# Query projection of a sparse attention: one 512-column matmul over high and low x in place of two of 256 columns

## The chip, the cores and the metric

The kernel runs on one core of one Trainium2 chip. Times are device microseconds of one launch. The core has TensorE (matmuls; PE in the profile, its weight loads PEld), VectorE (DVE), ScalarE (ACT), GpSimd (POOL) and SyncE (SP), which issues the DMAs. Each engine works off its own list of instructions in order; semaphores hold them together. PSUM, where matmuls write, has 8 banks of 512 fp32 columns on 128 partitions.

## The reference

A decoder layer on 256 tokens of width 2048, in fp32: an RMS norm, one wide projection, two attentions side by side (latent attention with 8 heads, sparse attention with 16 heads), an output projection, an MLP with squared ReLU, and a last norm. The change touches the projection that gives the sparse attention its queries, 16 heads of 64 features:

```python
n = rmsnorm(h, attn_norm_w[l])
proj = n @ w_in[l]
c_q, c_kv, k_rope, q_nsa, kv_cmp, kv_slc, kv_win, gate_logits = _split_cols(proj, IN_SIZES)
...
q = q.reshape(B, T, G, HG, NSA_DK)
```

so q_nsa is a product of 256 tokens x 2048 by 2048 x 1024. The norm's factor of a token is multiplied in afterwards, to the projected columns.

## The kernel before

Every fp32 product is made of three cheaper ones. A factor is split into a high part (rounded, type fp32r) and a low part (the rest), and high x high, high x low and low x high are summed in PSUM. ScalarE makes the high part of each chunk of weights (`split_hi`, L653), VectorE the low part (`split_lo`, L1010, which subtracts). Chunks of 2048 columns alternate between two places (`w_hi`, `w_lo`), so a chunk's splits wait for TensorE to be done with the chunk two before it (semaphore `w_used`, or `w_half` for half a chunk). x lies turned in SBUF as `xT[128, part, k, token]`, part 0 high and part 1 low.

The queries are made turned, with features on the partitions and the 256 tokens as columns: the weights are the stationary operand and xT moves. There are four parts of 256 features, each from two chunks of weights (8 blocks of k each), listed in `A_IN = (22, 24, 26, 28, 29, 30, 31, 32)`. The function `q_products` does a chunk in four quarters: a half of the blocks (4) and a half of the features (f). For each block it issues three matmuls of 256 columns: high weights with high x (L1896), high weights with low x (L1897), low weights with high x (L1900). Both halves of the features of a part sit side by side in one bank, and part p uses bank p.

The order of the work is the list `PLAN`, which each engine walks through, taking what is its own: ("hi", c) and ("lo", c) are splits of chunk c, ("w", c) is a whole chunk of matmuls and ("q", (c, n)) a quarter of one, ("s", i) a step of the attention, ("k", ...) single pieces. The chunks 21, 23, 25 and 27 (`CMP`) belong to the compression of keys and values and stand between query chunks. From chunk 29 on query quarters alternate with the first steps of the latent attention (scores in banks 4 and 5, turned probabilities in bank 6, results in bank 7); chunk 33 (`WO_M`) begins the output projection, which sums in banks 0 to 3.

Who uses banks 0 to 3 ahead of the queries: the turned keys stand in banks 0 and 1 and are split from there into `k2h` (ScalarE) and `k2l` (VectorE, semaphore `kv_out`, counts 3 and 4); the rotary query pieces stand in banks 2 and 3 and are split into `qs` (semaphore `qs_lo`, counts 1 and 2). A part leaves PSUM in `scale_queries`: VectorE multiplies the bank by `rrow`, the tokens' factors, into `qfa` or `qfb` (L1250, semaphore `q_in`). The pieces ("c", part) then split it into `q2a` or `q2b` (ScalarE L834, VectorE L1010). Parts 0 and 1 are scaled just ahead of their splits, parts 2 and 3 together in ("k", "out"), behind the last query chunk.

## Time and profile before

| | |
|---|---|
| median of 3 runs | 1027.6 us (1027.17 to 1027.95) |
| profiled execution, its own time | 1027.19 us |
| its span in the trace | 1025.4 us |
| TensorE busy | 1013.0 us, 99%, 5547 matmuls |
| weight loads | 879.2 us, 86% |
| VectorE busy | 793.4 us, 77% |
| ScalarE busy | 612.7 us, 60% |
| GpSimd busy | 88.9 us, 9% |
| query matmuls (L1896, L1897, L1900) | 3 x 128, from 117.2 to 181.1 us |

The span is the time from the first to the last instruction in the trace. Busy shares are an average over stages. A matmul's duration in the trace contains its way through the pipeline, so matmuls that follow each other overlap; the time that one takes from the next is the distance between their starts. A releaser (after <-) is the instruction whose semaphore event ended an engine's idle time.

### The profile page before, as it was taken

What the parts mean: (1) busy time and instruction counts of PE and PEld (TensorE: products, weight loads), DVE (VectorE), ACT (ScalarE), POOL (GpSimd) and SP (SyncE); (2) the same over time, 40 slices, a digit from 0 to 9 for tenths busy, and PEclk for the clock granted to TensorE, in tenths of its full rate; (3) what the DMA queues carried; (4) which work ended last, traced back from release to release, by engine and by line L of the source; (5) the groups of instructions that cost most, each with busy time, mean ns of one, the idle gap of its engine ahead of it and who ended that gap; (6) DMA issues with size and microseconds to landing.
All of it is one profiled execution on the core that took longest, in us unless ns stands there. A gap on an engine that the chain in (4) does not pass through costs nothing.

```text
span 1025.4 us, 14183 instructions
## 1 busy us (share of the span) xinstructions
PE 1013.0 (99%) x5547; PEld 879.2 (86%) x5547; DVE 793.4 (77%) x1086; ACT 612.7 (60%) x872; POOL 88.9 (9%) x151
## 2 busy tenths in 40 slices
PE   8999999999999999999999999999999999999996
PEld 7889999888888888888888888888888888888885
DVE  4655886988866589869958968976995996897594
ACT  5655855877764576556646655745655564575433
POOL 2135200632200000000000000000000000000002
PEclk9999999999999999999999999999999999999999
DMA  9576672243236547666666665666666666675553
GB/s 339 184 204 193 207 254 105 89 160 123 83 123 205 159 132 206 202 193 210 190 194 199 204 205 177 210 193 201 206 196 190 192 207 201 186 210 189 195 197 131
DMA packets 182798, 190.84 MB, mean 186 GB/s; under 512 B 9206, under 2 KB 145100, under 8 KB 182348
## 3 DMA queue, kind: packets, MB, share of 16 engines
q1 hardware_dynamic: 182300, 189.41, 58.5%
q8 instruction: 44, 0.72, 0.3%
q10 hardware_dynamic: 432, 0.52, 0.1%
q14 instruction: 22, 0.18, 0.0%
HBM read 187.82 MB, written 2.10 MB: 185 GB/s over the span
## 4 chain that ended last, share of the span: by engine, by line
PE 92%; DVE 4%; ACT 2%; DMA 1%; issue 1%; DVEq 0%; ACTq 0%
PE ps L2048 20%; PE ps L2116 12%; PE ps L2052 10%; PE ps L2123 6%; PE ps L1605 4%; PE ps L1606 4%; PE ps L1609 4%; PE ps L2091 4%; PE ps L2090 4%; PE ps L2097 4%; PE ps L2020 3%; PE ps L1896 2%; PE ps L1897 1%; PE ps L2025 1%; PE ps L1900 1%; PE ps L1880 1%
## 5 line engine op out<-in xcount | busy, mean ns | idle before, releaser
L2048 PE MATMUL ps<-xT,high 128*128 128x512 f32 x896 | 212.7, 390 | 0.2 <-DVE hid L1408 0.2
L2048 PEld LDWEIGHTS ps<-xT,high 128*128 128x128 f32 x896 | 168.0, 188 | 35.7 <-DVE hid L1408 1.0
L1010 DVE TENSOR_TENSOR low_even<-raw_even,high 128x2048 fp32r<-128x2048 f32 x60 | 137.3, 2289 | 57.7 <-ACT high L850 57.7
L850 ACT ACTIVATE high<-raw_even 128x2048 fp32r<-128x2048 f32 x60 | 114.8, 1914 | 83.9 <-DMA raw_even<-in_w_up 71.8
L1010 DVE TENSOR_TENSOR low_odd<-raw_odd,high 128x2048 fp32r<-128x2048 f32 (+1 forms) x60 | 122.5, 2041 | 27.0 <-ACT high L850 26.3
L2116 PE MATMUL ps<-high,hidT 128*128 128x512 f32 x544 | 135.4, 391 | 0.0
L2116 PEld LDWEIGHTS ps<-high,hidT 128*128 128x128 f32 x544 | 100.4, 188 | 19.8
L2052 PEld LDWEIGHTS ps<-xT,low_even 128*128 128x128 f32 x896 | 113.2, 188 | 4.4
L2052 PE MATMUL ps<-xT,low_even 128*128 128x256 f32 x896 | 114.3, 280 | 0.0
L850 ACT ACTIVATE high<-raw_odd 128x2048 fp32r<-128x2048 f32 (+1 forms) x60 | 102.6, 1711 | 12.2 <-DMA raw_odd<-in_w_down 10.8
L1010 DVE TENSOR_TENSOR w_lo<-raw_even,w_hi 128x1024 fp32r<-128x1024 f32 (+4 forms) x39 | 63.7, 1640 | 37.0 <-ACT w_hi L653 36.7
L1010 DVE TENSOR_TENSOR w_lo<-raw_odd,w_hi 128x1024 fp32r<-128x1024 f32 (+4 forms) x40 | 65.9, 1651 | 26.4 <-ACT w_hi L653 26.2
L653 ACT ACTIVATE w_hi<-raw_odd 128x1024 fp32r<-128x1024 f32 (+3 forms) x38 | 53.2, 1400 | 34.2 <-PE ps L1609 19.8
L653 ACT ACTIVATE w_hi<-raw_even 128x1024 fp32r<-128x1024 f32 (+3 forms) x37 | 51.0, 1383 | 31.0 <-PE ps L1609 21.2
L865 ACT ACTIVATE t_high<-t_sum 128x1024 fp32r<-128x1024 f32 x56 | 59.1, 1059 | 16.0 <-DVE t_sum L1360 8.2
L623 POOL TENSOR_TENSOR h_sb<-h_sb,fw 128x1024 f32<-128x1024 f32 x2 | 5.6, 2826 | 712.0 <-DMA fw<-in_final_norm_w 712.0
L2123 PE MATMUL ps<-low_odd,hidT 128*128 128x512 f32 x248 | 66.3, 390 | 0.0
L1010 DVE TENSOR_TENSOR t_low<-t_sum,t_high 128x2048 fp32r<-128x2048 f32 x28 | 64.0, 2285 | 0.9 <-ACT t_high L865 0.9
L892 ACT ACTIVATE s_part<-s_both 128x512 fp32r<-128x512 f32 x28 | 17.7, 632 | 77.6 <-DVE s_both L1395 77.6
L2123 PEld LDWEIGHTS ps<-low_odd,hidT 128*128 128x128 f32 x248 | 46.6, 188 | 9.7
L1605 PE MATMUL ps<-w_hi,yT 128*128 128x512 f32 x128 | 53.9, 421 | 0.3 <-DVE h_sb L1243 0.3
L882 ACT ACTIVATE hid<-ps 128x256 f32<-128x256 f32 x56 | 21.0, 375 | 51.2 <-PE ps L2052 51.2
(376 smaller groups left out, 2051.5 us busy)
## 6 DMA issues: line engine op xcount, KB each, us to landing
raw_even<-in_w_up SPq DMA_DIRECT2D x60, 1024.0 KB, 6.4
raw_odd<-in_w_down SPq DMA_DIRECT2D x32, 1024.0 KB, 5.2
raw_odd<-in_w_down SPq DMA_DIRECT2D x56, 512.0 KB, 4.6
raw_even<-in_w_o SPq DMA_DIRECT2D x8, 1024.0 KB, 5.2
raw_odd<-in_w_o SPq DMA_DIRECT2D x8, 1024.0 KB, 5.1
raw_odd<-in_w_in SPq DMA_DIRECT2D x6, 1024.0 KB, 5.3
raw_odd<-in_w_up SPq DMA_DIRECT2D x4, 1024.0 KB, 5.0
raw_even<-in_w_down SPq DMA_DIRECT2D x4, 1024.0 KB, 5.2
```

What stands on the lines that cost most here:

```text
L653: act.activation(span(w_hi[:, split_slot(c), :], c, half), span(raw(raw_slot(c)), c, half), ACT.Copy)\
L850: act.activation(high4[:, n % RAW, c0:2048], raw(n % RAW)[:, c0:2048], ACT.Copy).then_inc(done, 1)
L865: act.activation(t_high[:, s % 2, c], t_sum[:, s % 2, c], ACT.Copy).then_inc(sum_hi, 1)
L1010: return dve.tensor_tensor(dst, src, high.bitcast(F32), ALU.subtract)
L1605: pe.matmul(o, stationary(0, b, t), w_hi[:, slot, w], start=first, stop=False)
L1606: pe.matmul(o, stationary(0, b, t), w_lo[:, slot, w], start=False, stop=False)
L1609: m = pe.matmul(o, stationary(1, b, t), w_hi[:, slot, b * pitch + n0:b * pitch + n1], start=False, stop=last)
L2048: pe.matmul(ps[:, 0, :].rearrange("p (c t) -> p c t", c=2), high4[:, s, P * k:P * k + P], xT[:, :, k, :], start=k == 0, stop=False)
L2052: m = pe.matmul(bank(0, T), low4(s)[:, P * k:P * k + P], xT[:, 0, k, :], start=False, stop=k == KT - 1)
L2090: pe.matmul(bank(b), left[b](0), right[b](0), start=p == 0, stop=False)
L2116: pe.matmul(flat[:, c0:c0 + 512], of_hidden(part, 2 * p + b, t), high4[:, w, v], start=start and b == 0 and part == 0, stop=False)
L2123: m = pe.matmul(flat[:, c0:c0 + 512], of_hidden(0, 2 * p + b, t), low4(w)[:, v], start=False, stop=stop and b == 1)
```

## The change

For each block the matmuls of the high weights are joined: one matmul moves high and low x as one run of 512 columns, `xT[:, :, k, :]`, and writes a whole bank, products with high x in columns 0 to 255 and products with low x in 256 to 511. The low weights' matmul adds to the first half as before. So each half of a part's features takes a bank of its own: parts 0 and 2 use banks 0 and 1, parts 1 and 3 banks 2 and 3. A part now leaves PSUM in two steps, under the new kind ("e", part): ScalarE copies the second halves of both banks to SBUF (semaphore `q_cols`), VectorE adds the first halves to the copy and then multiplies by `rrow`. Part 2 gets a tile of its own, `qfc`.

Since parts share banks, TensorE's waits change: the first query chunk waits for both keys' banks, the third for both rotary banks, part 2 for the exit of part 0, part 3 for that of part 1, and the output projection's halves for the exits of parts 2 and 3.

```diff
@@ PLAN
+    PLAN += [("e", 0)] if _c == A_IN[2] else []
...
-    PLAN += [("lo", (_c + 1, None)), ("c", 0), ("k", "project"), ("c", 1)] if _s == 0 else []
-    PLAN += [("k", "small_values")] if _s == 4 else []
+    PLAN += [("lo", (_c + 1, None)), ("c", 0), ("k", "project"), ("e", 1), ("c", 1)] if _s == 0 else []
+    PLAN += [("k", "small_values"), ("e", 2)] if _s == 4 else []
...
-PLAN += [("k", "out"), ("s", NMLA)]
+PLAN += [("e", 3), ("s", NMLA)]
@@ ScalarE
+                elif kind == "e":
+                    act.wait_ge(w_used, A_IN[2 * i + 1] + 1)
+                    if i == 1:
+                        act.wait_ge(q_lo, 2)
+                    b = 2 * (i % 2)
+                    act.activation(queries(i)[1], ps[:, b:b + 2, T:2 * T], ACT.Copy).then_inc(q_cols, 1)
@@ VectorE, scale_queries
-                dve.wait_ge(w_used, A_IN[2 * part + 1] + 1)
-                if part == 1:
-                    dve.wait_ge(q_lo, 2)
-                dve.tensor_tensor(queries(part)[1], pairs(bank(part)), rrow[:, :].unsqueeze(1).broadcast_to((P, 2, T)), ALU.mult).then_inc(q_in, 1)
+                full, b = queries(part)[1], 2 * (part % 2)
+                dve.wait_ge(q_cols, part + 1)
+                link(dve.tensor_tensor(full, ps[:, b:b + 2, 0:T], full, ALU.add))
+                dve.tensor_tensor(full, full, rrow[:, :].unsqueeze(1).broadcast_to((P, 2, T)), ALU.mult).then_inc(q_in, 1)
@@ TensorE, q_products
-                    o = ps[:, part, T * f:T * f + T]
+                    both = ps[:, 2 * (part % 2) + f, :].rearrange("p (c t) -> p c t", c=2)
+                    o = bank(2 * (part % 2) + f, T)
...
-                        pe.matmul(o, w_hi[:, s, w], xT[:, 0, k, :], start=k == 0 and f == 0, stop=False)
-                        m = pe.matmul(o, w_hi[:, s, w], xT[:, 1, k, :], start=False, stop=False)
+                        m = pe.matmul(both, w_hi[:, s, w], xT[:, :, k, :], start=k == 0, stop=False)
...
-                        m = pe.matmul(o, w_lo[:, s, w], xT[:, 0, k, :], start=False, stop=k == KT - 1 and f == 1)
+                        m = pe.matmul(o, w_lo[:, s, w], xT[:, 0, k, :], start=False, stop=k == KT - 1)
@@ TensorE, the walk through PLAN (j is the place in A_IN)
-                    if j in (0, 2):
-                        pe.wait_ge(kv_out, 3 + j // 2)
-                    if j == 4:
+                    if j == 0:
+                        pe.wait_ge(kv_out, 4)
+                    if j == 2:
                         pe.wait_ge(qs_lo, 2)
+                    if j in (4, 6):
+                        pe.wait_ge(q_in, j // 2 - 1)
...
-                            pe.wait_ge(q_in, 2 * t + 2)
+                            pe.wait_ge(q_in, t + 3)
```

TensorE's order at its first query chunk, behind the compression chunk (`blk`). Before:

```order
643 L1926 MATMUL ps<-w_hi,blk 64x256
644 L1927 MATMUL ps<-w_lo,blk 64x256
645 L1896 MATMUL ps<-xT,w_hi 128x256 [waits half_lo,kv_out]
646 L1897 MATMUL ps<-xT,w_hi 128x256
647 L1900 MATMUL ps<-xT,w_lo 128x256
648 L1896 MATMUL ps<-xT,w_hi 128x256
```

And with the change:

```order
643 L1933 MATMUL ps<-w_hi,blk 64x256
644 L1934 MATMUL ps<-w_lo,blk 64x256
645 L1902 MATMUL ps<-xT,w_hi 128x512 [waits half_lo,kv_out]
646 L1905 MATMUL ps<-xT,w_lo 128x256
647 L1902 MATMUL ps<-xT,w_hi 128x512
648 L1905 MATMUL ps<-xT,w_lo 128x256
```

Three matmuls have become two, and the wait at row 645 is for a higher count of `kv_out`.

ScalarE's order where the last step of the latent attention ends and the first of the sparse one begins, before:

```order
131 L780 ACTIVATE prob,den<-prob,nmax 128x128 [waits score_m]
132 L781 ACTIVATE prob,den<-prob,nmax 128x256
133 L757 ACTIVATE probT<-ps 128x384 [waits o_t,pt_t]
134 L771 ACTIVATE ysb<-ps 128x256 [waits sq_sum,y_lo,o_t]
135 L773 ACTIVATE yT<-ysb,wcols 128x256 [waits y_out]
```

And with the change:

```order
134 L782 ACTIVATE prob,den<-prob,nmax 128x128 [waits score_m]
135 L783 ACTIVATE prob,den<-prob,nmax 128x256
136 L836 ACTIVATE qfb<-ps 128x512 [waits w_used]
137 L759 ACTIVATE probT<-ps 128x384 [waits o_t,pt_t]
138 L773 ACTIVATE ysb<-ps 128x256 [waits sq_sum,y_lo,o_t]
```

The copy of part 3 stands between the exponentials (L780 to L783) and the probability copy.

VectorE's order at the same place, before (yT is the remainder of an attention result, prob the masked scores):

```order
174 L1011 SCALAR_TENSOR_TENSOR yT<-ysb,wcols,yT 128x256 [waits y_hi]
175 L1250 TENSOR_TENSOR qfb<-ps,rrow 128x512 [waits w_used] x2
176 L1156 ISA prob,nmax<-ps,bias_even 128x128 [waits pt_t,bias_ok,score_t]
177 L1156 ISA nmax 128x1
178 L1156 ISA prob,nmax<-ps,bias_even 128x256
```

And with the change:

```order
178 L1019 SCALAR_TENSOR_TENSOR yT<-ysb,wcols,yT 128x256 [waits y_hi]
179 L1257 TENSOR_TENSOR qfb<-ps,qfb 128x512 [waits q_cols]
180 L1258 TENSOR_TENSOR qfb<-qfb,rrow 128x512 [waits dve_c]
181 L1164 ISA prob,nmax<-ps,bias_even 128x128 [waits pt_t,bias_ok,score_t]
182 L1164 ISA nmax 128x1
```

The scaling of two parts has become the add and the scaling of one; the add waits for ScalarE's copy.

## Rows read from the trace of the kernel before

**Rows 1.** The page: the span, and TensorE's busy time.

```profile
span 1025.4 us, 14183 instructions
...
PE 1013.0 (99%) x5547; PEld 879.2 (86%) x5547; DVE 793.4 (77%) x1086; ACT 612.7 (60%) x872; POOL 88.9 (9%) x151
```

**Rows 2.** Busy us by stage: length, PE, PEld, DVE, ACT, POOL, clock, DMA share, GB/s.

```profile
117.20:181.20 64.00, 64.00 (x539) 63.59 (x540) 48.97 (x95) 39.84 (x68) 3.47 (x4) 1.00 0.55 182
183.50:193.90 10.40, 10.25 (x57) 8.47 (x55) 8.55 (x34) 10.23 (x32) 8.46 (x24) 1.00 0.28 102
194.00:1000.00 806.00, 804.70 (x4173) 687.61 (x4174) 653.43 (x836) 481.14 (x666) 32.51 (x38) 1.00 0.59 184
```

**Rows 3.** Timeline (start, us, engine, line, op), TensorE, the first query chunk.

```profile
117.38 0.28 PE L1897 MATMUL ps<-xT,w_hi 128*128 128x256 f32 x1
...
123.01 0.28 PE L1926 MATMUL ps<-w_hi,blk 128*64 128x256 f32 x1
```

**Rows 4.** Timeline, TensorE, the MLP's first layer: a chunk, and the next one's start.

```profile
343.66 3.90 PE L2020 MATMUL ps<-xT,w_hi 128*128 128x512 f32 x16
347.40 2.08 PE L2025 MATMUL ps<-xT,w_lo 128*128 128x256 f32 x16
349.31 0.86 PE L2020 MATMUL ps<-xT,w_hi 128*128 128x512 f32 x3
```

**Rows 5.** Timeline, the last gelu step on VectorE and TensorE's transposes of it.

```profile
145.53 0.67 DVE L1269 SCALAR_TENSOR_TENSOR h1a<-h1b,h1c 30x512 f32<-30x512 f32 x1
...
146.29 0.43 PE L1969 MATMUL ps<-ident,h1a 30*128 30x30 f32 x4
```

**Rows 6.** Timeline, both key reads on VectorE; TensorE's step into the query chunk.

```profile
116.41 0.69 DVE L1010 TENSOR_TENSOR k2l<-ps,k2h 128x512 fp32r<-128x512 f32 x1
...
118.15 0.69 DVE L1010 TENSOR_TENSOR k2l<-ps,k2h 128x512 fp32r<-128x512 f32 x1
...
116.76 0.28 PE L1927 MATMUL ps<-w_lo,blk 128*64 128x256 f32 x1
117.16 0.38 PE L1896 MATMUL ps<-xT,w_hi 128*128 128x256 f32 x1
```

**Rows 7.** Timeline, VectorE's second read of the rotary pieces.

```profile
125.62 1.39 DVE L1010 TENSOR_TENSOR qs<-ps,qs 64x512 fp32r<-64x512 f32 x2
```

**Rows 8.** Chain of waits (start, us, what); L744's durations, min, median, max ns.

```profile
110.02 2.07 ACT knT L744 x4
...
L744 ACT ACTIVATE knT<-ps x4: 592/602/621, 110.0 to 111.5; 128x512 f32<-128x512 f32 x4
```

**Rows 9.** Timeline, VectorE where parts 2 and 3 are scaled; idle before in brackets.

```profile
184.91 1.28 DVE L1250 TENSOR_TENSOR qfb<-ps,rrow 128x512 f32<-128x512 f32 x2
...
186.10 0.28 DVE L1156 CUSTOM_DVE_ANT_0 prob<-ps,bias_even 128x128 f32<-128x128 f32 x1
...
187.87 0.48 DVE L1011 SCALAR_TENSOR_TENSOR yT<-ysb,wcols,yT 128x256 fp32r<-128x256 f32 x1
...
190.18 0.54 DVE L1011 SCALAR_TENSOR_TENSOR yT<-ysb,wcols,yT 128x256 fp32r<-128x256 f32 x1 [1.17 <-ACT yT L773]
```

**Rows 10.** Timeline, VectorE's half split of chunk 28, and TensorE's start on it.

```profile
137.17 1.22 DVE L1010 TENSOR_TENSOR w_lo<-raw_odd,w_hi 128x1024 fp32r<-128x1024 f32 x1
...
140.44 0.28 PE L1896 MATMUL ps<-xT,w_hi 128*128 128x256 f32 x1
```

**Rows 11.** Timeline, VectorE's mask of the fifth latent step.

```profile
168.20 0.29 DVE L1156 CUSTOM_DVE_ANT_0 prob<-ps,mask 128x128 f32<-128x128 f32 x1 [1.79 <-PE ps L1818]
```

**Rows 12.** Timeline, ScalarE's row ahead of the wait, and TensorE's wait for it.

```profile
185.56 0.47 ACT L757 ACTIVATE probT<-ps 128x384 f32<-128x384 f32 x1
...
193.44 0.37 ACT L771 ACTIVATE ysb<-ps 128x256 f32<-128x256 f32 x1
...
193.25 0.50 PE L1853 MATMUL ps<-ident,prob 128*128 128x128 f32 x3
193.95 0.67 PE L1880 MATMUL ps<-probT,v_sb 128*128 128x256 f32 x2 [0.21 <-ACT ysb L771]
```

**Rows 13.** Timeline, VectorE, a 512-column multiply beside GpSimd.

```profile
193.71 1.22 DVE L1187 TENSOR_TENSOR prob<-prob,scl 128x512 f32<-128x512 f32 x1
```

More of the change, by code:

```diff
@@ L171, in build @@
                                ("h1V", [P, 4, 2, NC], F32))
+        qfc, _ = seq(YN_AT, ("qfc", [P, 2, T], F32))
         KC_AT = YN_AT + 4 * 2 * 6 * T
@@ L316, in build @@
             "y_out", "y_sq", "y_hi", "y_lo", "sq_sum", "ysum_t", "ysum_ok", "yr_ok", "guessed")
-        merged, added, weighted, normed0, normed1, fsq, root_ok = sems(
-            "merged", "added", "weighted", "normed0", "normed1", "fsq", "root_ok")
+        merged, added, weighted, normed0, normed1, fsq, q_cols = sems(
+            "merged", "added", "weighted", "normed0", "normed1", "fsq", "q_cols")
         ht_t, ht_hi, ht_lo, hd_hi, hd_lo = sems("ht_t", "ht_hi", "ht_lo", "hd_hi", "hd_lo")
@@ L627, in queries @@
             high = (q2a, q2b)[part // 2][:, :, 2 * (part % 2):2 * (part % 2) + 2, :]
-            return high, qfa[:, :, :] if part < 2 else qfb[:, part % 2, :, :]
+            return high, (qfa[:, :, :], qfa[:, :, :], qfc[:, :, :], qfb[:, 1, :, :])[part]
         def sums_ready(eng, t, group, last):
@@ L1309, in _ @@
                     dve.wait_ge(rr_ok, 1)
-                elif i == "out":
-                    for part in (2, 3):
-                        scale_queries(part)
+                elif kind == "e":
+                    scale_queries(i)
                 elif kind == "c":
-                    if i < 2:
-                        scale_queries(i)
                     high, full = queries(i)
```

## The prediction

> **What bounds the kernel now.** I read the page first: TensorE is busy for 1013.0 of 1025.4 us [rows 1]. The change touches 117 to 194 us, so I asked for the stages next. From 117.2 to 181.2 us TensorE has no idle time at all (64.00 of 64.00), while VectorE is busy for 48.97 and ScalarE for 39.84, and the granted clock is 1.00. From 183.5 to 193.9 us ScalarE is busy for 10.23 of 10.40 us, and the chain of waits runs through it there [rows 2]. Busy matmuls overlap, so I took TensorE's time from start to start of its matmuls in the timeline. A change here pays only if it shortens TensorE's row of matmuls in the first stage or ScalarE's in the second, and any new wait of TensorE costs its full length, because nothing between these stages and the end has idle time to give back: from 194 to 1000 us TensorE is busy for 804.70 of 806 us.
>
> **Part 1, the merged matmul.** Eight chunks have 8 blocks of k and 2 halves each, so 128 triples of 256-column matmuls become 128 pairs, one of 512 columns and one of 256. The number of columns stays 768 per triple; one weight load in three goes. The price before: from the start at 117.38 to that at 123.01 us there are 47 matmuls, 119.8 ns each, 359 ns a triple [rows 3]. The price of the new shapes is in the first layer of the MLP, whose 512-column matmul moves the same tile in the same two-part form (high and low x side by side): 16 of them take 347.40 - 343.66 = 3.74 us, 233.8 ns each, and 16 of 256 columns take 1.91 us, 119.4 ns each [rows 4]. A pair costs 353.2 ns. Saved: 6.2 ns x 128 = 0.8 us. No row has the two shapes in alternation, so both ends: nothing saved if a 512 pays two surpluses of a 256; at the other end 768 columns at 2.4 GHz are 320 ns, each 256 now carries some 13 ns on top of 106.7, and a pair that keeps only one such surplus takes 333 ns and saves 26 ns x 128 = 3.3 us. I take 0.8, the nearest rows. One piece of it is lost again: at 146.29 us TensorE transposes what VectorE's last gelu step writes, and that ends at 145.53 + 0.67 = 146.20, so TensorE is there exactly in time [rows 5]; the one chunk before it gains 0.1 us for nothing. That leaves 0.7 us.
>
> The Trainium skill, page "TensorE: Matmul & The Clock Gate", section "Back-to-back issue gap", gives a warm isolated gap of N / 2.4 + 2.5 ns. By it one matmul fewer is worth 2.5 ns a triple, an estimate of 0.3 us in all, and the sum below would come out 0.4 us higher. The trace does not agree on the surplus (13 ns at 256 columns and 20 at 512, where the page has 2.5), so its sum stays aside.
>
> **Part 2, the first wait moves.** Part 0 of the queries used bank 0; now it uses banks 0 and 1 from its first matmul on. Both hold turned keys. Before, the first query chunk waited for kv_out 3 (bank 0 read) and the third for kv_out 4 (bank 1 read); now the first waits for 4. VectorE reads bank 0 at 116.41 to 117.10 us, then splits half a chunk, then reads bank 1 at 118.15 to 118.84. TensorE ends the compression chunk with a matmul that starts at 116.76, and starts the query chunk at 117.16, 0.06 us after the first read [rows 6]. It will start 0.06 us after the second, at 118.90: **1.74 us later**. VectorE has no idle time between 114 and 118.84 us and nothing that comes before these steps is changed, so the second read comes no earlier. Behind the waiting matmul stands the whole of TensorE's queue. Bounds: nothing, if TensorE found the time again later in waits that vanish; and 1.74, since the reads' times stand in the rows. I find nowhere to win it back: TensorE's stage up to 181.2 us has no idle time, and the splits of later weights are released by TensorE's own progress, so they shift with it. I take 1.74.
>
> **Part 3, the other new waits of TensorE.** Part 1 begins with the third query chunk, two query and two compression chunks after the first: 2 x 5.63 + 2 x 1.8 us behind 117.2, or near 132 us. It waits for banks 2 and 3, which hold rotary pieces that VectorE reads until 125.62 + 1.39 = 127.01 [rows 7]: 5 us to spare. Part 2 goes to banks 0 and 1 and waits for part 0's exit, which now stands on VectorE near 137 us; the part starts behind the transposes of 146.29 [rows 5]. Part 3 waits for part 1's exit, some 3 us of VectorE's work behind the first query's low half near 151 us, and starts two chunks behind part 2, with four steps of the attention between: later than 146.29 + 2 x 5.63 = 157.6 us. The output projection waits for q_in 3 and 4 in place of 2 and 4, and the fourth comes near 187.5 us, ahead of its first use at 190.40. All of these cost nothing; their cover is 5 to 10 us of other matmuls each, for the last about 3.
>
> **Part 4, the exits.** Each of the four parts gets one more ScalarE copy out of PSUM, 128x512, and one more VectorE operation. The nearest ScalarE row is the key copy, four in 2.07 us with 0.60 us for one: 0.49 us from one to the next [rows 8]. VectorE's scaling read from PSUM costs 0.60 us from one to the next (184.91 to 185.50, then 186.10) [rows 9]; it is now an add of such a read and a multiply behind a wait on the add, some 1.3 us. Part by part: exit 0 stands on VectorE between a chunk's splits and a piece of the keys; it moves the half split that starts at 137.17 to 138.5, and that ends at 139.7, while TensorE wants it at 140.44 [rows 10]. 0.7 us of cover remain. Exit 1 stands in the place of a scaling that is there already, and the first exit's departure frees 0.6 us ahead of it: free. Exit 2 takes 1.3 of VectorE's 1.79 us of idle time before 168.20 [rows 11], in a stretch where ScalarE is busy for two thirds [rows 2]: free.
>
> Exit 3 is the one that costs. On ScalarE it stands behind a step's exponentials and ahead of the probability copy that starts at 185.56 us [rows 12]. From there to the y copy at 193.44 us ScalarE has one operation behind another, and TensorE waits for that copy: its matmul at 193.95 us comes 0.13 us after the copy's end and 0.37 us later than the three transposes of 193.25 us with 0.11 us each would let it [rows 12]. So ScalarE's 0.49 us arrive at TensorE whole: **0.49 us**. On VectorE the add waits for ScalarE's copy, which ends near 186.15 us, where before both scalings were done at 186.10. The multiply ends near 187.5, and the masking of the first sparse scores starts 1.4 us late. Behind it VectorE has 1.17 us of idle time before 190.18 [rows 9], which itself moves 0.49 us out: 1.66 us of cover for 1.4, and only 0.26 left. Bounds of exit 3: nothing, if ScalarE's row has slack that the timeline hides; and 1.4 us, if VectorE's delay reaches TensorE instead. I take 0.49.
>
> **The sum.** 1.74 + 0.49 - 0.7 = +1.5 us. The profiled execution took 1027.19 us beside a span of 1025.4 [rows 1]; with the sum it is 1028.7. That execution lies 0.4 us under the median of the three runs (1027.6), so in their terms 1029.1. I put it at 1028.9, 0.13% above the median. What a measurement of this kernel can tell from no change is about 0.2%, 2.1 us: below 1025.5 is faster, above 1029.7 is slower.
>
> **Rivals**, with times in the terms of the three runs.
> - *VectorE's delay decides at the start of the output projection* (the slower side). The place is 186 to 194 us, the price 1.4 us in place of 0.49. It decides as soon as the add, the wait and the multiply take over 0.26 us more than I count, or the masking runs slower beside GpSimd, which is busy for 8.46 of the 10.40 us [rows 2]. For it: a 512-column multiply with both inputs in SBUF took 1.22 us at 193.71 [rows 13], while GpSimd worked, and the new multiply is of that kind; the scaling out of PSUM took half of that [rows 9]. Against it: the y remainder at 187.87 us has two inputs in SBUF too and took 0.48 us, no more than the 0.54 of its like at 190.18 [rows 9]. The Trainium skill, page "SBUF — State Buffer", section "Who interferes with whom", says that a VectorE instruction with two SBUF inputs contends with a GpSimd instruction that reads SBUF; by it the new multiply would take about twice its time and the rival would be the forecast. The trace bears it out at 193.71 and not at 187.87, so it gets a chance and no more. Sum 1.74 + 1.4 - 0.7 = +2.4; 1030.0, just slower.
> - *The pair packs tighter than its two shapes apart.* For it: a 512 carries 20 ns over its columns and a 256 only 13, so part of that may belong to like following like. Against: in 16 of a kind, the end of one run and the start of the next show no step of their own [rows 4]. At 333 ns a pair the sum is 1.74 + 0.49 - 3.3 = -1.1, 1026.5; halfway, 1027.7.
> - *The wait is given back.* TensorE late means VectorE and ScalarE ahead, which could erase the 0.37 us that it loses ahead of 193.95 [rows 12] and waits behind it. Against: ScalarE's row there is started by TensorE's own matmuls at 183.5. With the first wait worth nothing the sum is 0.49 - 0.7 = -0.2, 1027.4.
>
> That the change doesn't do what it says (two weight loads a pair) I leave out: the order shows the pairs.
>
> **How the numbers follow.** My forecast 0.52 (its own range 1028.1 to 1029.6), VectorE's delay 0.24, tighter packing 0.13, given back 0.07, the rest 0.04 (a collision that I do not see, either way). Slower: the second case and the upper edge of the first, 0.28. Faster: a fully tight pair, 0.03. Within 0.2%: 0.69. The range reaches from the two gaining cases' 1027.3 to 1030.5, a little over VectorE's price.
>
> **What would show it.** Right: the first query matmul starts near 118.9 us, behind VectorE's second key read, with some 1.9 us of TensorE waiting; 353 ns from pair to pair; TensorE's step at 193.95 comes near 195.5, still behind ScalarE's y copy. Wrong: pairs at 345 ns or less; a wait of TensorE for VectorE's masks or probabilities at 188 to 200 us; the start near 117.2; or a wait for q_in anywhere.

## The result, and the profile with the change

| | before | with the change |
|---|---|---|
| median of 8 runs each, us | 1027.68 (1027.17 to 1027.95) | 1030.62 (1030.06 to 1032.65) |
| ratio, 95% interval | | 1.0033, 1.0025 to 1.0042 |
| profiled execution, its own time; span | 1027.19; 1025.4 | 1030.6; 1028.8 |
| TensorE busy, matmuls | 1013.0, 5547 | 1013.4, 5419 |

The change makes the kernel 2.9 us slower. The forecast was 1028.9 us with a range up to 1030.5, so the direction of the sum was right and its size was not: 1.5 us were forecast, twice that came. Two of the eight executions with the change took 1032.6 us at a mean granted clock of 0.996, the six others 1030.06 to 1030.75 us at 0.998; the last section comes back to them.

The page with the change, to hold against [rows 1]: 128 matmuls and 6.4 us of weight loads are gone, and TensorE is busy no shorter.

```profile
span 1028.8 us, 13939 instructions
...
PE 1013.4 (99%) x5419; PEld 872.8 (85%) x5419; DVE 796.7 (77%) x1090; ACT 615.0 (60%) x876; POOL 90.7 (9%) x151
```

Busy times by stage don't place 3 us, so I read the starts of four of TensorE's matmuls in both timelines: the first of the queries, the first wide (256-column) `kh,qh` matmul of the last latent step (`kh` and `qh` are the high parts of the latent attention's keys and queries), and the first and last 256-column product with `vpad`, the padded values of the sparse attention.

| us | before | with the change | difference | forecast |
|---|---|---|---|---|
| last compression matmul to first query matmul | 0.40 | 2.13 | +1.73 | +1.74 |
| to the last latent step (the query stage) | 64.56 | 63.97 | -0.59 | -0.7 |
| to the first product with vpad (the turn) | 18.59 | 20.34 | **+1.75** | **+0.49** |
| to the last product with vpad | 98.49 | 98.46 | 0.0 | 0 |

The matmuls that bound the turn, before and with the change:

```profile
181.72 0.34 PE L1814 MATMUL ps<-kh,qh 128*128 128x256 f32 x1
200.31 0.60 PE L1880 MATMUL ps<-probT,vpad 128*128 128x256 f32 x2
```

```profile
184.02 0.33 PE L1819 MATMUL ps<-kh,qh 128*128 128x256 f32 x1
204.36 0.60 PE L1885 MATMUL ps<-probT,vpad 128*128 128x256 f32 x2
```

The sum is +2.9 us, the measured difference. What comes earlier and later contains nothing that was changed. Over the profiles of all fourteen kernels the part ahead differs by up to 1.7 us and the part behind by up to 0.7; between these two the differences are +1.16 and -0.6 us.

The timeline of TensorE at the first query chunk, with the change (start, us, engine, line, op, idle before and its releaser). It answers to [rows 3, 6]:

```profile
117.92 0.28 PE L1934 MATMUL ps<-w_lo,blk 128*64 128x256 f32 x1
120.05 0.50 PE L1902 MATMUL ps<-xT,w_hi 128*128 128x512 f32 x1 [1.85 <-DVE k2l L1018]
120.38 0.28 PE L1905 MATMUL ps<-xT,w_lo 128*128 128x256 f32 x1
120.50 0.40 PE L1902 MATMUL ps<-xT,w_hi 128*128 128x512 f32 x1
...
125.10 0.40 PE L1902 MATMUL ps<-xT,w_hi 128*128 128x512 f32 x1
```

and VectorE's second read of the keys, which lets it go:

```profile
119.31 0.68 DVE L1018 TENSOR_TENSOR k2l<-ps,k2h 128x512 fp32r<-128x512 f32 x1
```

The read ends at 119.99 and TensorE starts 0.06 us behind it. From 120.50 to 125.10 there are 13 pairs, 354 ns each, where 353 were forecast from [rows 4].

The third row of the table is the surprise. TensorE at the end of the turn, to hold against the two rows of [rows 12]:

```profile
196.04 0.49 PE L1858 MATMUL ps<-ident,prob 128*128 128x128 f32 x3
197.99 0.67 PE L1885 MATMUL ps<-probT,v_sb 128*128 128x256 f32 x2 [1.45 <-ACT ysb L773]
```

TensorE waits for the same copy of ScalarE as before, that of y, an attention result, out of PSUM (`ysb`). But that copy itself now waits, and not for ScalarE's own row. ScalarE:

```profile
187.86 0.58 ACT L836 ACTIVATE qfb<-ps 128x512 f32<-128x512 f32 x1
...
197.46 0.39 ACT L773 ACTIVATE ysb<-ps 128x256 f32<-128x256 f32 x1 [1.13 <-POOL sqacc L587]
```

GpSimd, with the change (cbias are the 16 constant-bias pieces of the sparse scores, vpad the padded values, sqacc the sum of y's squares, whose semaphore `sq_sum` the y copy waits for):

```profile
187.16 0.74 POOL L587 TENSOR_TENSOR sqacc<-sqacc,sq 128x256 f32<-128x256 f32 x1 [4.22 <-ACT sq L777]
187.86 6.89 POOL L608 TENSOR_SCALAR cbias<-cdist 128x30 f32<-128x30 f32 x16
194.69 0.99 POOL L611 MEMSET vpad<- 128x512 f32 x2
195.62 0.18 POOL L612 MEMSET pcs<- 128x96 f32 x1
195.75 0.74 POOL L615 COPY vpad<-kv_sb 128x256 f32<-128x256 f32 x2
196.46 2.02 POOL L587 TENSOR_TENSOR sqacc<-sqacc,sq 128x256 f32<-128x256 f32 x2
```

And the same row before the change:

```profile
184.85 0.74 POOL L585 TENSOR_TENSOR sqacc<-sqacc,sq 128x256 f32<-128x256 f32 x1 [4.25 <-ACT sq L775]
185.56 5.31 POOL L606 TENSOR_SCALAR cbias<-cdist 128x30 f32<-128x30 f32 x16
...
192.57 1.80 POOL L585 TENSOR_TENSOR sqacc<-sqacc,sq 128x256 f32<-128x256 f32 x2
```

GpSimd is never idle here, in either kernel. Before, the first of the two sums that start at 192.57 took 0.74 us and ended 0.13 us ahead of the y copy at 193.44 [rows 12], which showed no wait: two rows, ScalarE's and GpSimd's, arrived together. Counted from the wide `kh,qh` matmul, that sum ended after 11.59 us before and after 13.33 us with the change: GpSimd's row is 1.74 us later, the turn 1.75. With the change GpSimd's pieces take 6.89 us in place of 5.31. Two of the pieces carry most of it, and each starts just behind a VectorE operation with two inputs in SBUF. GpSimd:

```profile
189.25 0.80 POOL L608 TENSOR_SCALAR cbias<-cdist 128x30 f32<-128x30 f32 x1
193.57 1.18 POOL L608 TENSOR_SCALAR cbias<-cdist 128x30 f32<-128x30 f32 x1
```

The same line by itself (durations min/median/max in ns, first and last start):

```profile
L608 POOL TENSOR_SCALAR cbias<-cdist x16: 288/302/1184, 187.9 to 193.6; 128x30 f32<-128x30 f32 x16
```

VectorE:

```profile
188.47 0.69 DVE L1257 TENSOR_TENSOR qfb<-ps,qfb 128x512 f32<-128x512 f32 x1 [1.18 <-ACT qfb L836]
189.20 0.69 DVE L1258 TENSOR_TENSOR qfb<-qfb,rrow 128x512 f32<-128x512 f32 x1
...
193.38 1.23 DVE L1018 TENSOR_TENSOR w_lo<-raw_odd,w_hi 128x1024 fp32r<-128x1024 f32 x1
```

A piece has a median of 302 ns. The one beside the new multiply (L1258) took 0.80 us; the two that start during the add ahead of it (L1257, one input in PSUM) took 0.29 us each. With that and smaller delays the last piece came to start behind VectorE's half split of 193.38, and it took 1.18 us, until the split was done. Before the change the last piece started 0.16 us ahead of the split and took 0.39 us. GpSimd, before:

```profile
190.49 0.39 POOL L606 TENSOR_SCALAR cbias<-cdist 128x30 f32<-128x30 f32 x1
```

VectorE, before:

```profile
190.65 1.22 DVE L1010 TENSOR_TENSOR w_lo<-raw_odd,w_hi 128x1024 fp32r<-128x1024 f32 x1
```

### The profile page after: what moved, and what is told of

Its sections match the earlier page's. It is cut to its first block, busy times and chain, and to the rows that moved or that the text cites. A ratio compares the mean times of both kernels' runs of the same rounds, so it can differ in the third digit from the quotient of the medians.

```text
span 1028.8 us, 13939 instructions
## 1 busy us (share of the span) xinstructions
PE 1013.4 (99%) x5419; PEld 872.8 (85%) x5419; DVE 796.7 (77%) x1090; ACT 615.0 (60%) x876; POOL 90.7 (9%) x151
## 4 chain that ended last, share of the span: by engine, by line
PE 93%; DVE 4%; ACT 1%; POOL 1%; issue 1%; DMA 0%; DVEq 0%; ACTq 0%; POOLq 0%
PE ps L2055 20%; PE ps L2123 12%; PE ps L2059 10%; PE ps L2130 6%; PE ps L2098 4%; PE ps L2097 4%; PE ps L2104 4%; PE ps L1610 4%; PE ps L1611 4%; PE ps L1614 4%; PE ps L1902 3%; PE ps L2027 3%; PE ps L2032 1%; PE ps L1905 1%; PE ps L1885 1%; PE ps L1858 1%
## 5 line engine op out<-in xcount | busy, mean ns | idle before, releaser
L1611 PE MATMUL ps<-w_lo,yT 128*128 128x512 f32 x128 | 50.1, 392 | 0.0
```

Source lines behind the costliest of these rows:

```text
L1611: pe.matmul(o, stationary(0, b, t), w_lo[:, slot, w], start=False, stop=False)
```

## The experiments

All twelve in one table. Wait, query stage and turn are the stretches of the table above; pieces is GpSimd's time for the 16 pieces, longest the longest of them (all us, from one profile each). The ratio is to the kernel before on the same chip.

| | wait | query stage | turn | pieces, longest | median us | ratio (95%) |
|---|---|---|---|---|---|---|
| before | 0.40 | 64.56 | 18.59 | 5.31, 0.51 | 1027.68 | |
| the change | 2.13 | 63.97 | 20.34 | 6.89, 1.18 | 1030.62 | 1.0033 (1.0025 to 1.0042) |
| 1 first wait gone | 0.40 | 63.97 | 20.35 | 6.89, 1.18 | 1028.83 | 1.0012 (1.0003 to 1.0021) |
| 2 pieces a step earlier | 2.14 | 63.88 | 19.70 | 6.53, 1.50 | 1030.26 | 1.0026 (1.0016 to 1.0036) |
| 3 sum in PSUM | 2.13 | 65.33 | 19.11 | 5.11, 0.44 | 1029.74 | 1.0022 (1.0013 to 1.0030) |
| 4 before, with the wait | 2.13 | 64.54 | 18.63 | 5.33, 0.51 | 1029.13 | 1.0015 (1.0006 to 1.0024) |
| 5 exit 3 a step earlier | 2.12 | 63.91 | 19.39 | 5.76, 0.53 | 1029.61 | 1.0021 (1.0012 to 1.0030) |
| 6 before, ScalarE copy added | 0.39 | 64.56 | 19.13 | 5.18, 0.47 | 1027.90 | 1.0003 (0.9994 to 1.0012) |
| 7 before, SBUF multiply added | 0.40 | 64.58 | 22.19 | 6.66, 1.19 | 1031.04 | 1.0040 (1.0024 to 1.0055) |
| 8 before, PSUM multiply added | 0.39 | 64.57 | 18.61 | 4.96, 0.50 | 1027.55 | 0.9999 (0.9990 to 1.0008) |
| 9 three repairs | 0.40 | 63.76 | 19.85 | 6.41, 1.18 | 1028.29 | 1.0007 (0.9998 to 1.0016) |
| 10 as 9, multiply in SBUF | 0.40 | 63.82 | 20.62 | 6.71, 1.19 | 1029.54 | 1.0029 (1.0018 to 1.0041) |
| 11 first wait gone, sum in PSUM | 0.40 | 63.86 | 19.11 | 5.10, 0.44 | 1027.48 | 1.0000 (0.9991 to 1.0009) |
| 12 as 9, half split later | 0.40 | 63.57 | 19.68 | 5.51, 0.51 | 1027.99 | 1.0004 (0.9995 to 1.0013) |

**The first wait, from both sides (1 and 4).** Run 1 is the changed kernel with both key reads ahead of the split and the wait for bank 1's keys at the second half of the features:

```diff
-PLAN = [... ("keys", 0), ("hi", (CMP[0] + 1, 1)), ("lo", (CMP[0] + 1, 1)), ("keys", 1),
+PLAN = [... ("keys", 0), ("keys", 1), ("hi", (CMP[0] + 1, 1)), ("lo", (CMP[0] + 1, 1)),
@@ TensorE
-                        pe.wait_ge(kv_out, 4)
+                        pe.wait_ge(kv_out, 3)
@@ q_products
+                    if c == A_IN[0] and quarter == 1:
+                        pe.wait_ge(kv_out, 4)
```

> The changed kernel with both key reads ahead of the second half split of the first query chunk, and with the wait for the second read (kv_out 4) put ahead of the second quarter of that chunk alone. Theory (the first wait is lost whole): TensorE's wait of 1.85 us at the first query matmul goes, 1.7 us less than the changed kernel (1030.6), so 1028.9, and the loss near the start of the output projection stays. Rival (the wait is mostly given back later): 1030.0 to 1030.6.

Run 4 is the kernel before with only the wait of the change:

```diff
-                    if j in (0, 2):
-                        pe.wait_ge(kv_out, 3 + j // 2)
+                    if j == 0:
+                        pe.wait_ge(kv_out, 4)
```

> The kernel before with the first query chunk made to wait for the second key read, and nothing else. Theory (the wait costs its length): +1.74 us on 1027.7, so 1029.4. Rival (given back later): within 0.5 us of 1027.7.

TensorE's first query matmul in run 4:

```profile
117.62 0.28 PE L1927 MATMUL ps<-w_lo,blk 128*64 128x256 f32 x1
119.75 0.39 PE L1896 MATMUL ps<-xT,w_hi 128*128 128x256 f32 x1 [1.85 <-DVE k2l L1010]
```

The wait alone makes the kernel before 1.4 us slower by the medians (1029.13 beside 1027.71), without it the change is 1.8 us faster, and in the profiles nothing of it is given back or grows later: the turn is 18.63 in run 4 and 20.35 in run 1. The wait's term was right.

**What in exit 3 costs (3, 6, 7, 8).** Run 3 is the change with the sum written back to PSUM, so that the multiply has one input in SBUF and not two:

```diff
-                link(dve.tensor_tensor(full, ps[:, b:b + 2, 0:T], full, ALU.add))
-                dve.tensor_tensor(full, full, rrow...
+                link(dve.tensor_tensor(ps[:, b:b + 2, 0:T], ps[:, b:b + 2, 0:T], full, ALU.add))
+                dve.tensor_tensor(full, ps[:, b:b + 2, 0:T], rrow...
```

> The changed kernel with the exits' sum written back to PSUM, so that the multiply that follows has one input in SBUF and one in PSUM in place of two in SBUF; the count and order of instructions are the same. Theory A (the multiply itself holds up GpSimd): the cbias piece that took 0.8 us beside it falls to 0.3, GpSimd's 16 pieces take 6.4 in place of 6.9 us, 0.5 us less in all: 1030.1. Theory B (all of GpSimd's stretch stems from it, the later overlap with the half split included): 5.3 us and 1029.0. Rival (contention plays no part): 6.9 us and 1030.6.

The turn falls from 20.34 to 19.11 us and the pieces to 5.11, as theory B had it; the time, 1029.74 us, is 0.7 above its number. The y copy shows no wait for GpSimd, and TensorE's is 0.20 us:

```profile
189.77 5.11 POOL L608 TENSOR_SCALAR cbias<-cdist 128x30 f32<-128x30 f32 x16
...
198.66 0.67 PE L1885 MATMUL ps<-probT,v_sb 128*128 128x256 f32 x2 [0.20 <-ACT ysb L773]
```

What is left over the kernel before, 0.52 us, is the 0.49 us of ScalarE's row that the prediction gave to the whole exit. (This profile's query stage is 65.33 us because its granted clock fell behind the first wait, which the last section shows; run 11 has the same products and exits and 63.86, so that is not the edit.) Runs 6 to 8 put the operations one by one into the kernel before, unused: a ScalarE copy at ("k", "out"), or a third multiply behind VectorE's two scalings, once out of `v_sb` in SBUF and once out of PSUM.

```diff
+                    act.activation(qfc[:, :, :], v_sb[:, 0, 0:512].rearrange(...), ACT.Copy)          # run 6
+                    dve.tensor_tensor(qfc[:, :, :], v_sb[:, 0, 0:512].rearrange(...), rrow..., ALU.mult)  # run 7
+                    dve.tensor_tensor(qfc[:, :, :], pairs(bank(3)), rrow..., ALU.mult)                # run 8
```

> The kernel before with one more ScalarE copy of 128x512 (SBUF to SBUF, 0.6 us) where the changed kernel has part 3's; its result is not used. Both theories, the prediction's and that of GpSimd's row, say +0.4 to +0.5 us: from the eighth latent step to the first product with vpad 19.0 to 19.1 us in place of 18.6, 1028.1 to 1028.2. If ScalarE's row had slack there: 18.6 us.

> The kernel before with one more VectorE multiply of 128x512, both inputs in SBUF, behind the scaling of parts 2 and 3; its result is not used. VectorE has 1.17 us of idle time behind it. Theory (two inputs in SBUF hold up GpSimd's cbias, which then reaches into VectorE's half split): GpSimd's 16 pieces take 6 to 6.9 us in place of 5.3, the stretch to the first vpad product 19.4 to 20.2 us in place of 18.6. Rival (VectorE's lateness alone counts, and its idle time covers 0.6 us): 18.6 us and no change.

> As the kernel with the extra VectorE multiply of two SBUF inputs, but with one input in PSUM (bank 3, the same length); its result is not used. Theory: GpSimd's 16 pieces stay at 5.1 to 5.4 us and the stretch at 18.6 us. Rival (any more work of VectorE there costs): the same loss as with two inputs in SBUF.

Runs 7 and 8 are the cleanest pair. The same multiply, in the same place and with nearly the same duration on VectorE (0.74 and 0.68 us), costs nothing out of PSUM (turn 18.61) and 3.6 us of turn out of SBUF. Run 7, GpSimd and TensorE:

```profile
186.03 6.66 POOL L607 TENSOR_SCALAR cbias<-cdist 128x30 f32<-128x30 f32 x16
...
196.38 0.93 PE L1882 MATMUL ps<-probT,v_sb 128*128 128x256 f32 x2 [2.17 <-ACT ysb L772]
```

and run 8, GpSimd:

```profile
186.71 4.96 POOL L607 TENSOR_SCALAR cbias<-cdist 128x30 f32<-128x30 f32 x16
```

The expectation of 0.8 to 1.6 us for run 7 was too small. The wait for y is 2.17 us; a further 1.6 us is TensorE's clock, which the last section shows. Run 6 costs 0.54 us of turn, as ScalarE's row should (in time it can't be told from nothing).

**Moving GpSimd's row (2).** The pieces are issued one step of the attention earlier:

```diff
-                if i == NMLA:
+                if i == NMLA - 1:
                     pool.wait_ge(w_used, WO_M)
...
+                if i == NMLA:
```

> The changed kernel with GpSimd's 16 cbias multiplies one step earlier, ahead of its sum of squares of that step, so that they begin when the last query chunk is done. Theory (GpSimd's row of cbias, memsets, copies and sums of squares is what the y copy waits for; VectorE's new operations stretch it by 1.7 us): TensorE's wait of 1.45 us at the L1885 matmul near 198 us goes or falls to what ScalarE's row leaves (0.2 to 0.9), so 1.2 to 1.7 us less than the changed kernel, 1028.9 to 1029.4. Rival (ScalarE's or VectorE's own delay is the cause, as in the prediction): 1030.3 to 1030.6, no change.

It missed: 1030.26 us is the rival's number. The wait for y is gone, but the turn is only 0.64 us shorter, and from the turn's end to the last product with `vpad` TensorE takes 0.57 us longer than in the changed kernel. The pieces now start beside a whole split, and GpSimd's later work holds VectorE up. GpSimd:

```profile
182.95 6.53 POOL L608 TENSOR_SCALAR cbias<-cdist 128x30 f32<-128x30 f32 x16 [0.82 <-PE ps L1906]
...
190.12 0.99 POOL L612 MEMSET vpad<- 128x512 f32 x2
```

VectorE:

```profile
181.44 2.84 DVE L1019 TENSOR_TENSOR w_lo<-raw_even,w_hi 128x2048 fp32r<-128x2048 f32 x1
184.94 0.29 DVE L1187 TENSOR_SCALAR prob<-prob,scl 128x128 f32<-128x128 f32 x1
...
190.31 1.01 DVE L1187 TENSOR_SCALAR prob<-prob,scl 128x128 f32<-128x128 f32 x1
...
193.44 1.76 DVE L1019 TENSOR_TENSOR w_lo<-raw_odd,w_hi 128x1024 fp32r<-128x1024 f32 x1
```

The same scaling takes 0.29 us at 184.94 and 1.01 us at 190.31, where GpSimd's memsets run; the half split takes 1.76 in place of 1.23. Part of the loss had changed engines.

**Moving the exit (5, 9, 10).** Run 5 puts ("e", 3) ahead of the step before, for all engines:

```diff
+    PLAN += [("e", 3)] if _s == NMLA - 2 else []
     PLAN += [("s", _s + 1)]
...
-PLAN += [("e", 3), ("s", NMLA)]
+PLAN += [("s", NMLA)]
```

> The changed kernel with part 3's exit one step earlier in the order of all engines, ahead of the eighth latent step: ScalarE's copy falls into its 2.2 us of idle time, VectorE's add and multiply are done before GpSimd's cbias row begins. Theory (exit 3 costs 1.7 us by ScalarE's row, by VectorE's lateness and by GpSimd beside them): from the eighth latent step's matmuls to the first product with vpad TensorE takes 18.6 us as before the change, not 20.3; 1.7 us less, 1028.9. Rival (exit 3's work costs wherever it stands, since VectorE's and ScalarE's rows are full there): 19.1 us or more, 1029.4 to 1030.6.

It missed: a turn of 19.39 and 1029.61 us are what the rival had. The y wait is gone (pieces 5.76), but VectorE's add and multiply now stand ahead of the last latent mask, and TensorE waits for that:

```profile
186.51 0.50 PE L1842 MATMUL ps<-k2h,q2a 128*128 128x512 f32 x1 [0.98 <-DVE nmax L1166]
```

Runs 9 and 10 therefore move ScalarE's copy alone, by a PLAN entry of its own, and contain run 1's edit; 9 also has run 3's.

```diff
+    PLAN += [("copy", 3)] if _s == NMLA - 2 else []
     PLAN += [("s", _s + 1)]
@@ ScalarE
-                elif kind == "e":
+                elif kind == "copy" or (kind == "e" and i < 3):
```

> The changed kernel with all three losses taken up: the second key read ahead of the half split (as in the run without the first wait), the add of a part written back to PSUM so that the multiply has one SBUF input, and ScalarE's copy of part 3 one step earlier, before step 7 of the attention, while VectorE's add and multiply stay before step 8. Theory (first wait 1.73, streaming gain 0.59, exit 3 made of 0.5 us of ScalarE's row plus the stretched GpSimd row): the wait is 0.40 us, the query stage 63.97, GpSimd's constant-bias pieces take about 5.1 us and from the query stage's end to the first product with v it is 18.6 us as before; the time is 0.6 us below the kernel before: 1027.0 to 1027.2 if the kernel before gives 1027.7, ratio 0.9994. Rival (the exit costs ScalarE's 0.5 us wherever its copy stands, since the step before is as full): stretch 19.1, time 1027.6, ratio 1.0000.

> The same without the sum in PSUM: first wait gone, ScalarE's copy of part 3 one step earlier, VectorE's add and multiply before step 8 and the multiply with both inputs in SBUF. Theory (contention of the multiply with GpSimd is a term of its own, about 1.2 of exit 3's 1.75 us): GpSimd's constant-bias pieces take 6 to 7 us, TensorE waits over 1 us for the y copy behind GpSimd's sum, stretch 19.4 to 19.8, time 1028.0 to 1028.4. Rival (once ScalarE's copy is out of the way, VectorE runs earlier, beside less of GpSimd's row, and the multiply costs nothing): pieces about 5.3 us, stretch 18.6, time as the run with all three, 1027.1.

The difference of the two goes the way that was expected: 0.77 us of turn, where 1.23 came with the copy at its first place (run 1 against run 11). So the SBUF multiply costs time at either place of the copy, but not the same. The medians differ by 1.25 us; three of run 10's seven executions are of the kind with a lower mean clock, which the last section describes. With the multiply still in SBUF, moving the copy gains nothing: the turn is 20.62 us, beside 20.35 in run 1. The level is not: run 9's turn is 19.85 us, where theory had 18.6 and its rival 19.1. With the copy out of the way VectorE is 0.6 us earlier against the first query matmul than in run 11, and starts its half split before GpSimd's last piece. GpSimd, run 9:

```profile
191.15 1.18 POOL L610 TENSOR_SCALAR cbias<-cdist 128x30 f32<-128x30 f32 x1
```

VectorE, run 9:

```profile
190.96 1.23 DVE L1020 TENSOR_TENSOR w_lo<-raw_odd,w_hi 128x1024 fp32r<-128x1024 f32 x1
```

The piece itself is later too, by 0.3 us. An earlier VectorE made a later TensorE.

**The two repairs that hold (11).** Run 1's and run 3's edits together, the copy where the change has it.

> First wait gone and the sum in PSUM, ScalarE's copy of part 3 where the change puts it. Theory: what is left is the streaming gain of 0.59 us against 0.5 us of ScalarE's row: wait 0.40, query stage 63.97, stretch 19.1, time level with the kernel before, 1027.6, ratio 1.0000. Rival (the sum in PSUM makes the query stage longer, as its profile with the clock at 0.996 read 65.33): query stage 65 and time 1028.7.

As expected: 1027.48 beside 1027.35 us of the kernel before in the same comparison. The gain of 0.7 us in the query stage and the 0.52 us of ScalarE's row nearly cancel.

**The collision moved (12).** Run 9 with VectorE's half split of chunk 34 behind the four masks that follow it:

```diff
-                if kind == "lo":
+                if kind == "lo" and i != (WO_M + 1, 0):
                     split_lo(*i)
@@ VectorE's slot, behind masked(...)
+                if i == NMLA + 2:
+                    split_lo(WO_M + 1, 0)
```

> The run with all three losses taken up lost 1.26 us more than expected at the output projection's start: GpSimd's 16th constant-bias piece started at 191.15, beside VectorE's half split of 190.96 to 192.19, and took 1.18 us in place of 0.29; where the piece starts before the split (the kernel before: 190.49, split 190.65) it takes 0.39. This kernel is that one with the half split moved behind the four masks that follow it on VectorE. Theory (a piece that starts beside a long VectorE operation with two SBUF inputs lasts as long as that operation; the collision is one of place, and the last piece decides): no piece over 0.6 us, all 16 in 5.2 to 5.5 us, TensorE waits 0.2 to 0.5 us for the y copy, stretch 18.5 to 18.9 us, time 1.0 us below that run, ratio to the kernel before 0.9997. Rival (the split meets GpSimd's later memsets, copies and sums wherever it stands, and they lose what the pieces gain): pieces 5.3 us, but the y copy as late as before, stretch 19.5 to 19.9, ratio 1.0007.

The rival had it: the turn is 19.68 us and the time level with run 9's. No piece is longer than 0.51 us and all take 5.51 us, so the collision was that of piece and split; but the split, now at 191.02 to 192.24, meets the copies to `vpad`. GpSimd, run 12:

```profile
184.88 5.51 POOL L610 TENSOR_SCALAR cbias<-cdist 128x30 f32<-128x30 f32 x16
...
191.39 1.45 POOL L617 COPY vpad<-kv_sb 128x256 f32<-128x256 f32 x2
192.81 2.02 POOL L589 TENSOR_TENSOR sqacc<-sqacc,sq 128x256 f32<-128x256 f32 x2
```

The two copies took 0.74 us in the changed kernel and take 1.45 here; TensorE waits 1.26 us for y. No version of the twelve is measurably faster than the kernel before.

## Why the prediction was wrong

- **What bounds it:** right that a wait of TensorE in 117 to 194 us costs its full length and is not won back (in some executions it costs more, by the clock: see the last section), and that a gain must come out of its row: the 1.73 and the 0.59 us both arrive. Wrong that ScalarE's row alone bounds the turn.
- **Part 1, the pairs:** right. 354 ns a pair, 0.59 us gained in the profile of the change and 0.6 to 1.0 in runs 1 and 9 to 12; the tighter packing did not come. TensorE's transposes at 148.96 us, at VectorE's last gelu step ending at 148.90, were the small loss named.
- **Part 2, the first wait:** right, 1.73 for 1.74 us.
- **Part 3, the other waits:** right. Between 120.5 and 186 us no wait of TensorE is listed.
- **Part 4, exits 0 to 2:** right by the same listing.
- **Part 4, exit 3:** this step failed. Its term was 0.49 us and measured 1.75. The two-SBUF multiply, through GpSimd, is what makes it larger: without it the turn is 1.23 us shorter (20.34 against 19.11 in run 3; 20.35 against 19.11 from run 1 to 11), and the 0.52 us left are ScalarE's copy, as worked out (runs 3, 6, 11). These two are not links of one chain: the rows run side by side and the later one decides. GpSimd's alone is 1.74 us late, all of the 1.75, and hides ScalarE's 0.49. "From there to the y copy at 193.44 us ScalarE has one operation behind another" was true, but the copy has a second releaser, `sq_sum`, and GpSimd's row ended just as late. I had GpSimd busy for 8.46 of 10.40 us in [rows 2] and did not follow its row to the y copy. Its bound of 1.4 us was for another way and too low.
- **The rival "VectorE's delay"** named the right operation and the wrong victim. It looked for the multiply to become slow; it took 0.69 us, as fast as one out of PSUM. Who was slow was GpSimd. The 1.22 us at 193.71 us, the evidence for this rival, was indeed contention (the sixteen operations of that line, L1187, have a median of 0.68 us), but it began while GpSimd's sum of 193.46 us was under way, and there VectorE was the one held up.
- The argument against that rival was a misreading of the same kind. The y remainder at 187.87 us took its normal 0.48 us [rows 9], and I concluded that there was no contention. Its other side stands in GpSimd's row of the kernel before, but it is small: the piece that starts within it, at 188.16, took 0.33 us where the median is 0.29. The longest, 509 ns at 188.56, stands beside two scalings of probabilities (L1178 at 188.46 and L1179 at 188.66), which read one tensor in SBUF; so operations with two SBUF inputs are not the only ones beside which a piece is long.

```profile
L606 POOL TENSOR_SCALAR cbias<-cdist x16: 287/292/509, 185.6 to 190.5; 128x30 f32<-128x30 f32 x16
```

The Trainium skill, page "SBUF — State Buffer", section "Who interferes with whom", says that a VectorE instruction with two SBUF inputs contends with GpSimd instructions that read SBUF, that the ports are an exclusive lock, and that the order of issue decides who blocks. Runs 7 and 8 agree with the first (pieces of 6.66 against 4.96 us), the pieces of 1.18 us beside a split of 1.23 with the second, and run 2 with the third: there GpSimd came first and VectorE took 1.01 us for 0.29. I had quoted only the first and looked for it on one side.

How long a piece takes follows from where it starts, in the pieces of before, the change and eight of the runs (2, 3, 5, 7 to 11). One that starts over 0.06 us into a VectorE operation with two SBUF inputs ends 0.14 to 0.17 us behind that operation's end, whatever the operation's length:

| GpSimd's piece starts, takes | beside VectorE's | which ends | piece ends behind it |
|---|---|---|---|
| before, 188.16, 0.33 | y remainder | 188.35 | 0.14 |
| before, 190.49, 0.39 | y remainder | 190.72 | 0.16 |
| change, 189.25, 0.80 | multiply L1258 | 189.89 | 0.16 |
| change, 191.78, 0.42 | y remainder | 192.06 | 0.14 |
| change, 193.57, 1.18 | half split | 194.61 | 0.14 |
| run 2, 182.95, 1.50 | whole split | 184.28 | 0.17 |

A piece that was under way when such an operation began is not held by it, and of those that start in its first 0.06 us some are held and some are not: 0.29 us at 190.24 before the change, 0.80 at 189.25 with it.

Not settled: whether the turn can be brought to 18.6 us with the exit in it. The exit moved as a whole (run 5), ScalarE's copy moved (9, 10), VectorE's half split moved (12) and GpSimd's pieces moved (2) were tried, but not a version in which GpSimd does the sum that the y copy waits for ahead of the pieces.

## What to carry to other kernels

Before an operation is priced by its own engine's row, look at what its operands lock: a VectorE operation with two SBUF inputs beside a busy GpSimd costs on GpSimd's row, and an intermediate left in PSUM avoids it at no cost on VectorE (add and multiply 0.70 and 0.69 us in run 3, 0.69 and 0.69 in the change). Where a critical wait has several releasers, follow each one's row back and write down its slack; a chain shows only the last, and a second row, here one that ended 0.13 us ahead of the copy, takes over with the first small change. With two rows that close, moving work earlier can make it collide and end later.

## What the hardware showed that I had not expected

A 0.7 us operation can cost 3.6 us. In run 7 TensorE's wait of 2.17 us was followed by slow matmuls. By stretches of run 7 (length, PE, PEld, DVE, ACT, POOL busy, granted clock, DMA share, GB/s):

```profile
190.00:194.50 4.50, 4.20 (x23) 3.36 (x21) 3.92 (x15) 3.97 (x13) 4.44 (x11) 1.00 0.00 0
196.40:200.20 3.80, 3.80 (x12) 3.11 (x13) 2.31 (x3) 3.45 (x13) 3.41 (x4) 0.55 0.00 0
200.20:204.00 3.80, 3.80 (x26) 3.38 (x25) 2.64 (x9) 3.05 (x9) 0.00 (x0) 1.00 0.00 0
```

The granted clock averaged 0.55 of full speed over the 3.8 us behind the wait, most of them at the lower of its two levels, 1.2 GHz, and 12 matmuls ran where 26 did in the next stretch. TensorE, run 7, the same 512-column matmul in both stretches:

```profile
198.39 0.63 PE L1607 MATMUL ps<-w_hi,yT 128*128 128x512 f32 x1
...
202.41 0.40 PE L1607 MATMUL ps<-w_hi,yT 128*128 128x512 f32 x1
```

In the profile of the changed kernel the waits of 1.85 and 1.45 us were not followed by it, nor was that of 2.23 us in run 10's, longer than this one: behind all three the granted clock reads 1.00. But the same first wait of 1.85 us was followed by it in the profile of run 3, whose kernel is the changed one up to there. TensorE, run 3, the 512-column query matmul at the lower and at the full clock:

```profile
121.85 0.63 PE L1902 MATMUL ps<-xT,w_hi 128*128 128x512 f32 x1
...
125.40 0.39 PE L1902 MATMUL ps<-xT,w_hi 128*128 128x512 f32 x1
```

The granted clock was 0.50 from 122 to 124 us there, the pairs came 0.64 us apart in place of 0.35, and the query stage took 65.33 us in place of some 63.9. So it is not a property of the kernel alone: one wait of one length was followed by the lower clock in one execution and not in another.

The times of the unprofiled executions point the same way. In the changed kernel and in runs 2, 3, 4, 5, 7 and 10 TensorE's longest wait between 117 and 200 us is 1.85 to 2.23 us; 14 of their 59 executions have a mean granted clock of 0.995 or 0.996. In the changed kernel these two took about 2 us more than the others, in run 10 three took 1031.44 to 1032.08 us beside 1028.71 to 1029.54. In runs 1, 6, 8, 9, 11 and 12, whose longest wait there is 1.46 us, none of 64 executions has so low a mean, nor has any of the 95 of the kernel before that were measured beside the runs. Where the clock was low in an unprofiled execution is not on record, and what decides whether a wait is followed by it was not tried.
